# VectorE's order in the local attention units: reading the projection's bank ahead of the maxima

## The reference, cut to what matters

```python
proj = jnp.einsum('bsd,dc->bsc', x, w_in)
q_s, k_s = apply_rope(q_s), apply_rope(k_s)      # 8 query heads, 2 key heads of 64
s = jnp.einsum('bnqhgd,bnkhd->bnhgqk', qb, kk) * scale      # window of 128, blocks of 128
m = jnp.maximum(jnp.max(s, axis=-1, keepdims=True), sink)
e = jnp.exp(s - m)
p = e / (jnp.sum(e, axis=-1, keepdims=True) + jnp.exp(sink - m))
out = jnp.einsum('bnhgqk,bnkhd->bnqhgd', p, vv)
```

## Time and profile before

| what | us |
|---|---|
| median of 3 runs (lowest, highest) | 679.45 (679.43, 679.52) |
| the profiled execution, its own time | 679.46 |
| its span on the core | 677.7 |
| TensorE matmuls busy in the span | 665.8 |
| VectorE busy | 540.3 |
| ScalarE busy | 392.2 |
| GpSimd busy | 50.8 |

### The profile page before, as it was taken

One profiled execution on the slowest core, in us unless ns is written; L12 is line 12 of the kernel. 1 busy time (PEld: TensorE's weight loads), 2 busy tenths in 40 slices (PEclk: granted clock), 3 DMA queues, 4 the chain that ended last, 5 costly groups with the idle time before them and its releaser, 6 DMA issues.

```text
span 677.7 us, 10965 instructions
## 1 busy us (share of the span) xinstructions
PE 665.8 (98%) x4034; PEld 594.8 (88%) x4034; DVE 540.3 (80%) x1021; ACT 392.2 (58%) x728; POOL 50.8 (7%) x74
## 2 busy tenths in 40 slices
PE   8999999999999999999999999999999999999995
PEld 6977888888888888888899999999999998888884
DVE  5579998767876226655989998888998889998888
ACT  5669687467766244524436555554554558767740
POOL 2102111111001011110200000000000000000000
PEclk9999999999999999999999999999999999999999
DMA  8236667876512886886021244334334327987302
GB/s 314 78 116 171 186 176 213 216 183 164 121 63 95 317 205 168 220 270 200 0 79 60 102 150 155 104 128 155 110 122 155 127 92 249 372 258 208 108 31 93
DMA packets 29560, 107.38 MB, mean 158 GB/s; under 512 B 3616, under 2 KB 3744, under 8 KB 26784
## 3 DMA queue, kind: packets, MB, share of 16 engines
q1 hardware_dynamic: 24624, 79.60, 34.1%
q0 software_dynamic: 4896, 27.28, 16.6%
HBM read 104.77 MB, written 25.17 MB: 192 GB/s over the span
## 4 chain that ended last, share of the span: by engine, by line
PE 89%; DVE 5%; ACT 2%; issue 2%; DMA 1%; POOL 0%; DVEq 0%; SPq 0%; ACTq 0%
PE ps L1643 12%; PE ps L1645 12%; PE ps L1644 12%; PE ps L1960 10%; PE ps L1962 10%; PE ps L1961 10%; PE ps L2028 5%; PE ps L2030 5%; PE ps L2029 5%; PE ps L1720 2%; PE ps L1706 2%; ACT rope L659 1%; PE ps L1681 1%; PE ps L1676 1%; DVE sl L982 1%
## 5 line engine op out<-in xcount | busy, mean ns | idle before, releaser
L982 DVE TENSOR_TENSOR sl<-raw,sh 128x1024 fp32r<-128x1024 f32 x46 | 56.3, 1225 | 43.6 <-ACT sh L643 43.5
L1960 PE MATMUL ps<-hTh,sh 128*128 128x256 f32 x320 | 90.6, 283 | 0.0
L1961 PE MATMUL ps<-hTh,sl 128*128 128x256 f32 x320 | 90.6, 283 | 0.0
L1962 PE MATMUL ps<-hTl,sh 128*128 128x256 f32 x320 | 90.6, 283 | 0.0
L1643 PE MATMUL ps<-xh,sh 128*128 128x512 f32 x208 | 83.6, 402 | 1.1 <-DVE q_f L1049 1.1
L1645 PE MATMUL ps<-xl,sh 128*128 128x512 f32 x208 | 81.3, 391 | 0.0
L1644 PE MATMUL ps<-xh,sl 128*128 128x512 f32 x208 | 81.1, 390 | 0.0
L643 ACT ACTIVATE sh<-raw 128x1024 fp32r<-128x1024 f32 x46 | 48.9, 1064 | 35.6 <-PE ps L1645 22.5
L1960 PE MATMUL ps<-vt,sh 128*128 128x256 f32 x240 | 68.1, 284 | 0.2 <-ACT sg L883 0.2
L1962 PE MATMUL ps<-vt,sh 128*128 128x256 f32 x240 | 67.9, 283 | 0.0
L1961 PE MATMUL ps<-vt,sl 128*128 128x256 f32 x240 | 67.9, 283 | 0.0
(11 more groups left out here) (255 smaller groups left out, 1747.6 us busy)
## 6 DMA issues: line engine op xcount, KB each, us to landing
raw<-in_slabs SPq DMA_DIRECT2D x46, 512.0 KB, 4.3
raw_f_even<-in_gu SPq DMA_DIRECT2D x10, 1280.0 KB, 5.4
raw_f_odd<-in_gu SPq DMA_DIRECT2D x10, 1280.0 KB, 5.4
item_raw<-tw SPq DMA_DIRECT2D x44, 256.0 KB, 3.1
item_raw<-in_wdn SPq DMA_DIRECT2D x33, 256.0 KB, 5.6
tw<-in_wdn POOLq DMA_DIRECT2D x11, 512.0 KB, 5.6
tw<-tw POOLq DMA_DIRECT2D x22, 256.0 KB, 4.4
x_raw<-in_xT SPq DMA_DIRECT2D x8, 256.0 KB, 5.8
```

Source lines behind the costliest of these rows:

```text
L982: dve.tensor_tensor(slot(sl, n, w), raw_of(n), slot(sh, n, w).bitcast(F32), ALU.subtract).then_inc(lo_ready, 1)
L1960: pe.matmul(dst, sh[:, w], bh[:, c, :], start=start and c == 0, stop=False, skip_group_check=True)
L1961: pe.matmul(dst, sl[:, w], bh[:, c, :], start=False, stop=False, skip_group_check=True)
L1962: last = pe.matmul(dst, sh[:, w], bl[:, c, :], start=False, stop=c == KC // 2 - 1, skip_group_check=True)
```

## The change

In steps 7 to 14 VectorE takes the bank of the slab before (`take(n - 1)`) ahead of the maxima and not behind them. There are no local maxima in step 14, so the order differs in steps 7 to 13, units 1 to 7. In step 5 the low part of slab 8 is left out at the step's end and made in step 6 behind unit 0's maxima. No instruction is added or removed, and the streams of ScalarE, GpSimd, SyncE and TensorE are the same.

```diff
@@ -1335,8 +1335,13 @@
             for n in range(1, N_WOUT + KC - WOUT_TAIL + 1):
+
+                if N_QF < n <= N_V:
+                    take(n - 1)
                 for a in units_at(n, 0):
                     maxima(a)
+                if n == N_QF:
+                    slab_lo(n - 1 + AHEAD)
                 if n - 1 in N_QS:
                     rope_cosine(n - 1, N_QS.index(n - 1))
                 if n == N_QS[-2] + 1:
@@ -1347,7 +1352,8 @@
                     forget_logits()
                     rotate_keys()
                     slab_lo(n - 1 + AHEAD)
-                take(n - 1)
+                if not N_QF < n <= N_V:
+                    take(n - 1)
                 for a in units_at(n, 2):
                     sum_o(a)
                 if n == N_CUM + 1:
@@ -1370,7 +1376,8 @@
                     merge(n - 1 - N_WO)
                 if n - 1 in N_QS[:2]:
                     rope_add(N_QS.index(n - 1))
-                if n != N_VK[1]:
+
+                if n not in (N_VK[1], N_QF - 1):
                     slab_lo(n + AHEAD)
```

## The result

| | us |
|---|---|
| changed kernel, median of 6 runs (lowest, highest) | 682.15 (681.8, 682.7) |
| kernel before, median of 6 runs beside and ahead of it (lowest, highest) | 679.44 (678.89, 680.29) |
| ratio, 95% interval | 1.004 (1.0028 to 1.0053) |
| span of the changed kernel's profiled execution | 680.4 |

The change makes the kernel 2.7 us slower; 681.9 was forecast. The spans differ by the same 2.7 (680.4 and 677.7). In the changed kernel the lines behind L1340 stand seven higher: scores L1683 and L1688, values L1727.

What follows compares the result with a forecast made beforehand. TensorE, busy nearly all of the span, was taken as the bound, with 2.8 us winnable at its waits. Values of unit 6 2.3 later plus 0.1 for slower first matmuls, on 679.46, gave 681.9 us; range 680.8 to 683.0.

Steps and rivals of the forecast that it cites:

- The bound of 2.8 us: TensorE's waits in the local units: three for q_f, 2.07 together, and 0.74 at unit 1's scores; nothing winnable elsewhere.
- The slab's move: Slab 8's low part behind unit 0's maxima: unit 1's scores 0.74 earlier, ScalarE's rotation 2.05 earlier.
- the chain of the maxima: Forecast starts of VectorE's maxima, units 1 to 7, each summed from the one before: 53.75 to 105.35.
- The take ahead of the maxima: Steps 7 to 13: waiting take delays maxima, exponentials and scores; values of unit 6 start 2.3 later, at 108.9.
- the neighbourhood that I had named as unknown: On VectorE, maxima followed by the o sum, not in the trace; 1.65 taken, 1.49 the other length seen.
- The 0.4 more: Upper allowance over six steps for unseen VectorE neighbourhoods, at most 0.13 more a step; likeliest case 681.0 to 682.4.
- The first: Rival, faster: takes come in time, all four stalls go and no new one comes; 676.7 us, chance 0.06.
- The second: Rival, no change: kh_f steps run at TensorE's 8.12, values of unit 6 wait at most 1 us; 679.3 to 680.6, chance 0.10.
- The third: Rival, worse: the lag goes on behind slab 14, each further microsecond costing one; 683 to 684 us, chance 0.06.
- The sign list at the end of the prediction: Profile signs: no q_f wait, scores wait for exponentials, unit 6's values for ptl 1.0 or more, slab 14 at 109.9.
- the ring: Steps 11 to 13: maxima, exponentials, slab hi, kh_f, take wait in a circle; 8.36 and 8.88 against TensorE's 8.12.

Runs made afterwards that it cites:

- with three: Kernel with slab 8's low part alone moved, plus low parts of slabs 11 and 12 made behind ptl in steps 9 and 10: 678.26 us, ratio 0.9969.
- first run: Against the changed kernel, every take put back behind the maxima, so only slab 8's low part is moved: 677.07 us, ratio 0.9953.
- the extra copies: Changed kernel plus one 64 x 512 copy on ScalarE ahead of kh_f in each of steps 11 to 13: 685.03 us, ratio 1.0072.

## Why the prediction was right, point by point

**What bounds the kernel.** The bound of 2.8 us for what can be won was right to about 0.1. With one slab moved 1.97 came, with three 2.72, and about 0.2 was left at slab 9.

**The slab's move.** Maxima of unit 0 were forecast near 42.5 and came at 42.61; scores of unit 1 near 47.7, and came at 47.88. The rotation was to start 2.05 earlier, at 46.4; it started at 46.54. In words I counted only the 0.74 of unit 1's wait as this part's gain; the 2.0 by which ScalarE starts earlier stood in the chain of the maxima. Alone the part is worth 2.0 (first run), since every q_f behind it comes earlier.

**The take ahead of the maxima.** The forecast starts of the maxima against the measured ones:

| unit | forecast | measured |
|---|---|---|
| 1 | 53.75 | 53.86 |
| 2 | 62.7 | 62.63 |
| 3 | 71.5 | 71.38 |
| 4 | 79.75 | 79.76 |
| 5 | 88.1 | 88.13 |
| 6 | 97.0 | 97.12 |
| 7 | 105.35 | 105.60 |
| values of unit 6 | 108.9 | 109.30 |

The mechanism is right, and the closeness of the numbers is in part luck: the steps missed by up to 0.19 either way (unit 1 to 2 was forecast 8.96 and took 8.77, unit 3 to 4 8.25 and 8.38), and the errors cancel to 0.03 at unit 5.

The 0.4 at the end have two sources. The changed kernel's profile is 0.15 later at its kl_s already. The rest is the neighbourhood that I had named as unknown: behind kl_f the maxima take 1.77 to the o sum (88.13 to 89.90), where I had 1.66, since they start with a gap of 0.38 and not 0.27 between their first two. Two more lengths differed, with opposite signs: maxima followed by ptl took 1.49 (53.86 to 55.35, forecast 1.65), and a slab followed by the take 1.25 (59.95 to 61.20, forecast 1.13). The 0.4 more that the prediction allowed for this over six steps does not follow from its own 0.13 a step, which gives 0.8; the take stands right behind the slab on the path in only two of the steps, those to units 3 and 4.

**The rivals.** The first needed kh_f to be done before VectorE gets there; VectorE waited 0.62, 0.54 and 0.62 for it, where I had 0.7. The second, that the kh_f steps keep TensorE's pace, failed by 0.87 and 0.36 us in two steps. The third would show as a wait behind slab 14; there is none, and the spans differ by 2.7 as the values did by 2.68.

**The sign list at the end of the prediction.** Waits for the exponentials were forecast at units 2, 3, 4, 6 and 7. The view shows them at 2, 3, 4 and 7. Unit 6's is there as pace: 8.48 behind unit 5 where 8.12 is free. So is one at unit 5, 8.38 behind unit 4, which the list did not have. Values of unit 6 were to wait 1.0 or more, and waited 1.31. Slab 14 was to start at 109.9 in place of 107.5; it started at 110.29, where the kernel before has 107.51.

## What to carry to other kernels

When an instruction that waits for another engine is moved ahead of one that this engine waits for, write down the closed chain that results, with every instruction that stands in between on either queue, and compare its length with the step of the engine that bounds the kernel. A chain that is a few per cent too long costs nothing in the first step and everything in the last; engines that are 58% and 80% busy over the whole run, or 80% and 87% in the steps of the ring, as ScalarE and VectorE here, don't speak against it. Try the parts of a change apart: here one was worth 2 us and the other hid it.

## What the runs showed of the hardware

Executions of one kernel differ by up to 3.9 us (676.16 to 680.06 with three slabs), and three profiles show where: in the first 40 us. The granted TensorE clock there was 1.00 in the profile of the slab's move alone, 0.96 when the same kernel was run again and 0.91 with three slabs; from 40 to 500 us it is 1.00 in all three. kl_s starts at 39.49, 41.58 and 42.97, and from there to the end of the span it is 635.9, 635.8 and 635.3 us. The first stretch of each (us, then busy time of each engine, granted clock, DMA share, GB/s), in the order of the clock:

```profile
0.00:40.00 40.00, 38.59 (x208) 33.21 (x209) 24.55 (x37) 25.98 (x38) 7.64 (x19) 1.00 0.54 188
```

```profile
0.00:40.00 40.00, 37.13 (x199) 32.00 (x200) 23.98 (x36) 23.93 (x35) 7.66 (x19) 0.96 0.51 184
```

```profile
0.00:40.00 40.00, 37.48 (x191) 31.79 (x192) 22.70 (x35) 23.05 (x33) 7.65 (x19) 0.91 0.49 175
```

A low mean is a part of the stretch at the lower of the two levels, 1.2 GHz. In the second and third execution it lies between 5 and 15 us (0.87 and 0.78, then 0.82 and 0.50, by stretches of 5 us), behind waits of TensorE for a slab's high part, the longest 1.52 and 1.01 us. In the first execution TensorE's longest wait from 5 to 15 us was 0.23. The wait alone does not decide it, since the kernel before waited 1.05 us there and kept 1.00. What made it differ between executions of the same kernel was not tried. For a change of 1 us it means that the time between two events inside one profile tells more than the whole.

A wait of TensorE can also be followed by a lower clock, and that I had not reckoned with. That the wait is the cause is read from the order in time and was not tried apart. In the changed kernel, with waits of up to 1.31 us open, the granted clock stays at 1.00 from 40 us to slab 15. With the extra copies it also stays there behind a wait of 1.36 us at the scores of unit 7 (103.50). Behind the 1.79 us of the run with the extra copies it fell to 0.50 (1.2 GHz) and cost 1.6 us (above). With the takes alone the scores of unit 2 waited 2.00 us, until 59.55, and the clock fell as well:

```profile
57.00:60.00 3.00, 0.99 (x6) 0.57 (x5) 2.92 (x8) 2.51 (x10) 0.90 (x1) 1.00 0.58 161
...
62.00:64.00 2.00, 2.00 (x6) 1.52 (x6) 1.96 (x4) 1.71 (x3) 0.81 (x1) 0.50 0.09 16
64.00:66.00 2.00, 2.00 (x13) 1.67 (x12) 1.97 (x8) 0.54 (x2) 0.00 (x0) 0.84 0.84 287
```

There it cost nothing in the end. TensorE was late by it: the scores of unit 3 started 4.80 us behind unit 2's maxima (64.59 to 69.39), against 3.73 in the changed kernel (62.63 to 66.36). But VectorE needed no scores that early: the maxima of units 1 to 3 start 8.77 and 8.75 us apart (55.82, 64.59, 73.34), as in the changed kernel. From the values of unit 6 on, where TensorE alone sets the pace, the fall was paid in full.
